# Decode tokens taken one block apart per stage, their attention on VectorE, a token-major mLSTM, and a weight stream of four split slots behind two raw ones

## The reference

```python
def hybrid_mixer(xn, conv_state, C0, n0, m0, w_in, b_in, conv_w, g_mh, w_out, chunk):
    proj = xn @ w_in + b_in
    gb, gc, hc, q, k, v, o, gates = jnp.split(proj, splits, axis=-1)
    y_conv, new_conv = short_conv(gc * hc, conv_state, conv_w)
    y_conv = gb * y_conv
    ...
    h, (C, n, m) = mlstm(qh, kh, vh, ig, lf, C0, n0, m0, chunk)
    h = h * lax.rsqrt(jnp.mean(h * h, axis=-1, keepdims=True) + EPS)
    y_ml = jax.nn.sigmoid(o) * (h * g_mh)
    out = jnp.concatenate([y_conv, y_ml], axis=-1) @ w_out
...
        hp = hp + mp
        hp = hp + cross_attn(rmsnorm(hp, g_cross[l]), pk, pv, w_xq[l], w_xo[l])
        hp = hp + swiglu(rmsnorm(hp, g_ffn[l]), w_gu[l], w_down[l])
```

## Time and profile before

| | |
|---|---|
| median of 3 runs | 3322.16 us (3309.95 to 3325.18) |
| the profiled execution | 3309.95 us |
| its span, first to last instruction | 3308.1 us |
| busy share: TensorE products, weight loads | 95%, 88% |
| VectorE, ScalarE, GpSimd | 51%, 39%, 45% |
| HBM traffic | 378.18 MB read, 13.30 MB written, 118 GB/s |

### The profile page before, as it was taken

The page is one execution under the profiler, slowest core; times in us unless marked ns, Lnnn a source line. Parts: engine busy times, 40 slices in busy tenths (PEclk is TensorE's granted clock), DMA queues, the critical chain, the costliest instruction groups (busy, mean ns, idle before and its releaser), DMA issues.

```text
span 3308.1 us, 42531 instructions
## 1 busy us (share of the span) xinstructions
PE 3148.3 (95%) x16970; PEld 2918.7 (88%) x16970; DVE 1671.9 (51%) x2695; ACT 1281.6 (39%) x2056; POOL 1489.7 (45%) x614
## 2 busy tenths in 40 slices
PE   8889999999899999889999998999999999999998
PEld 7888799988879999888799998888999888688886
DVE  6677532277754224677542267764224666542224
ACT  5444343344334334444343344344334444332222
POOL 1344355653434555434255553334655433244443
PEclk9999999999999999999999999999999999999999
DMA  5334233343423333334233343333333332122222
GB/s 211 108 123 142 90 122 126 128 137 120 136 97 118 124 130 124 129 129 142 79 126 127 128 143 120 117 122 117 126 128 124 131 121 90 52 94 97 96 102 89
DMA packets 132795, 394.24 MB, mean 119 GB/s; under 512 B 19812, under 2 KB 42340, under 8 KB 132472
## 3 DMA queue, kind: packets, MB, share of 16 engines
q1 hardware_dynamic: 99632, 350.87, 30.6%
q10 hardware_dynamic: 32968, 40.66, 3.9%
HBM read 378.18 MB, written 13.30 MB: 118 GB/s over the span
## 4 chain that ended last, share of the span: by engine, by line
PE 76%; DVE 14%; ACT 4%; issue 3%; DMA 2%; ACTq 1%; DVEq 0%; POOL 0%; SPq 0%
PE gb L312 67%; PE ta L473 2%; DMA o_sn<-work 1%; DVE r_res L1198 1%; DVE big L1091 1%; DVE big L1150 1%; DVE work L1114 1%; DVE work L1173 1%; PE tb L495 1%; PE td L495 1%; PE gm L505 1%; PE ta L521 1%; DVE x L1003 1%; ACT work L789 1%; DVE x L1189 1%
## 5 line engine op out<-in xcount | busy, mean ns | idle before, releaser
L294 POOL TENSOR_TENSOR w_lo<-w_raw,w_hi 128x1024 fp32r<-128x1024 f32 x610 | 1489.5, 2446 | 1791.8 <-ACT w_hi L604 1791.4
L312 PE MATMUL gb<-xn_hi,w_hi 128*128 128x386 f32 (+1 forms) x3280 | 1182.7, 361 | 15.5 <-DVE big L998 14.1
L312 PE MATMUL gb<-xn_hi,w_lo 128*128 128x386 f32 (+1 forms) x3280 | 1153.3, 352 | 0.0
L312 PE MATMUL gb<-xn_lo,w_hi 128*128 128x386 f32 (+1 forms) x3280 | 1152.8, 351 | 0.0
L604 ACT ACTIVATE w_hi<-w_raw 128x1024 fp32r<-128x1024 f32 x623 | 657.9, 1057 | 1223.3 <-PE gb L312 1171.5
L312 PEld LDWEIGHTS gb<-xn_hi,w_hi 128*128 128x128 f32 x3280 | 625.3, 191 | 51.2 <-issue 17.7
L312 PEld LDWEIGHTS gb<-xn_lo,w_hi 128*128 128x128 f32 x3280 | 625.4, 191 | 31.3 <-issue 2.2
L312 PEld LDWEIGHTS gb<-xn_hi,w_lo 128*128 128x128 f32 x3280 | 624.6, 190 | 26.2
L312 PE MATMUL gb<-act_hi,w_hi 128*128 128x386 f32 (+2 forms) x1648 | 575.8, 349 | 28.4 <-DMA mats<-mats_d 12.2
L312 PE MATMUL gb<-act_hi,w_lo 128*128 128x386 f32 (+2 forms) x1648 | 570.7, 346 | 0.0
L312 PE MATMUL gb<-act_lo,w_hi 128*128 128x386 f32 (+2 forms) x1648 | 570.7, 346 | 0.0
(11 more groups left out here) (199 smaller groups left out, 2476.3 us busy)
## 6 DMA issues: line engine op xcount, KB each, us to landing
w_raw<-w_st SPq DMA_DIRECT2D x610, 512.0 KB, 3.4
big<-kvc_d ACTq DMA_DIRECT2D x32, 512.0 KB, 4.5
big<-rows_d SPq DMA_DIRECT2D x16, 580.0 KB, 5.1
w_raw<-w_kv SPq DMA_DIRECT2D x16, 512.0 KB, 4.4
x<-x_blk SPq DMA_DIRECT2D x8, 772.0 KB, 6.9
y<-x ACTq DMA_DIRECT2D x16, 386.0 KB, 6.5
big<-x_blk ACTq DMA_DIRECT2D x24, 193.0 KB, 3.2
big<-rows_d SPq DMA_DIRECT2D x4, 768.0 KB, 5.2
```

Of the source, the lines that this page charges most:

```text
L294: pool.tensor_tensor(w_lo[:, g % NS, :], w_raw[:, g % NR, :], w_hi[:, g % NS, :].bitcast(F32), ALU.subtract).then_inc(w_lo_done, 1)
L312: mm = pe.matmul(gb[:, s, 0:wd], a[:, s, k * P:(k + 1) * P], r[:, k, 0:wd], start=(first and k == ks[0] and i == 0), stop=(last and k == k ...
```

## The change

- **Decode tokens.** All 8 go together, and one block later per stage: through the mixer's projections with block 1 (`DM`), its output and the queries with block 2 (`DO`), attention output and FFN with block 3 (`DX`). So each stage has one block of 392 columns, three of 384 and one of 512. Their mLSTM state update is done on VectorE and TensorE in block 1's FFN. Their attention is done on VectorE in block 2's FFN: 32 pieces (`dec_piece`), each a multiplication over 1,024 elements per partition and a sum, with the cache (1 MB for two pieces) and the broadcast query or probability rows loaded by SyncE between the weights.
- **Gates.** The two gate groups become one; a product with `pick` separates the forget gates. The four output-gate groups move ahead of the heads, with a sigmoid on ScalarE, so a block has 121 groups. The rows of the scans are turned into columns by `turn_rows`.
- **mLSTM token-major.** Numerator and normaliser come as 128 tokens by 129 columns: `n_part` has three products in place of five, the state is 129 columns wide with one update, the normaliser is one column per chunk, and `h_turn` transposes the result once per chunk, within the next head's q group.
- **Inputs scaled ahead.** `next_scale` multiplies the next block's input by the inverse norm in the third part of the FFN, so mixer groups need only a bias and ScalarE evacuates q, k, v, one convolution group and the gates (`take`).
- **Attention.** The steps of heads 2 and 3 move between the parts of the first three `O_XO` groups (`xo`); three output groups of the mixer are opened at once.
- **Slots.** `w_hi` and `w_lo` get 4 slots, `w_raw` 2, the product banks stay 3 (`NP`). The loads of the next block's input and the stores of `y` go from ScalarE's queue to SyncE's.

```diff
-BLK = [(3, 2), (3, 2), (3, 2), (3, 2), (4, 0)]
...
 NB = len(BLK)
+DM, DO, DX = 1, 2, 3
...
 O_GATE = 0
-O_HEAD = 2
-PER_HEAD = 7
+O_SIG = 1
+O_HEAD = O_SIG + HEADS
+PER_HEAD = 6
 O_OUT = O_HEAD + HEADS * PER_HEAD
...
-NS = 3
-NR = 3
+NS = 4
+NP = 3
+NR = 2
...
+G1, G2 = O_FF[1] - O_FF[0], O_FF[2] - O_FF[0]
+PIECE_AT = [2 * f + 1 for f in range(1, 8)] + [16 + m for m in range(8)] + [G1 + 1]
+PIECE_AT += [G1 + 11, G1 + 13] + [G1 + 14 + m for m in range(8)] + [G2 + 2 * f + 1 for f in range(6)]
...
+            def cache(i):
+                if i >= 2:
+                    sp.wait_ge(piece_done, 2 * (i - 2) + 2)
+                sp.dma_start(dcache[:, i % 2, :], kd_d[i] if i < NDEC else vd_d[i - NDEC]).then_inc(cache_loaded[i % 2], 16)
...
+            def piece_row(i):
+                if i >= 2:
+                    sp.wait_ge(piece_done, i - 1)
+                t, j = (i // 2) % NDEC, i % 2
+                if i < 2 * NDEC:
+                    src = qrow_d.rearrange("(k t) d -> t k d", t=NDEC)[t:t + 1, 4 * j:4 * j + 4, :].to_broadcast([P, 4, P])
+                    sp.dma_start(dbuf[:, j, :].rearrange("p (k d) -> p k d", k=4), src).then_inc(row_loaded[j], 16)
+                else:
+                    src = prow_d.rearrange("(t j) c -> t (j c)", t=NDEC)[t:t + 1, j * 512:(j + 1) * 512].to_broadcast([P, 512])
+                    sp.dma_start(dbuf[:, j, :], src).then_inc(row_loaded[j], 16)
...
+                if off == O_HEAD + 7 and b:
+                    store_y(b - 1)
...
+                    sp.wait_ge(y_lo, b * 8 + 8)
+                    for k in range(0, KT, 4):
+                        sp.dma_start(x_next[:, k:k + 4, 0:w],
+                                     x_blk[(b + 1) * KT + k:(b + 1) * KT + k + 4, :, 0:w].rearrange("k p c -> p k c")).then_inc(xnext_loaded, 16)
...
+                if b == DO:
+                    place = off - O_FF[0]
+                    if place == 0:
+                        sp.wait_ge(o_lo, b * 8 + 8)
+                        cache(0)
+                        cache(1)
+                    if place == 1:
+                        sp.wait_ge(qrow_stored, 16)
+                        piece_row(0)
+                        piece_row(1)
+                    for i in range(2, 4 * NDEC):
...
+                            if i >= 3:
+                                cache((i + 1) // 2)
+                    for i in range(2, 4 * NDEC):
+                        if place == max(PIECE_AT[i - 2] + 5, PROW_AT if i >= 2 * NDEC else 0):
+                            if i == 2 * NDEC:
+                                sp.wait_ge(prow_stored, 16)
+                            piece_row(i)
...
+                def pick_f():
+                    read_out(pe, gw(b, O_GATE))
+                    pe.matmul(td[:, 0:w_mix(b)], pick, gi[:, 0:w_mix(b)], start=True, stop=True).then_inc(f_picked, 1)
...
+                def turn_rows():
+                    pe.wait_ge(rows_exp, b + 1)
+                    for i, row in enumerate((a_row, row_g, row_e)):
+                        for c in range(CH):
+                            a = (i * CH + c) * HEADS
+                            mm = pe.matmul(tb[:, a:a + HEADS], row[:, c * P:(c + 1) * P], ident[:, 0:P:32], start=True, stop=True)
+                    mm.then_inc(col_t, 1)
...
+                def n_part(h, c):
...
+                    pe.matmul(bank[:, V1:2 * V1], w_sb[:, s, :], ktv[:, s, P:P + V1], start=True, stop=True)
+                    pe.matmul(bank[:, 2 * V1:3 * V1], ktv[:, s, 0:P], vs_sb[:, s, :], start=True, stop=True).then_inc(bu_done, 1)
+                    if c:
+                        pe.wait_ge(upd_done, j)
+                    elif b:
+                        pe.wait_ge(upd_done, ch0(b - 1, h + 1))
+                    old = state[:, h, :] if c == 0 else ws[:, c % 2, :]
+                    pe.matmul(bank[:, 0:V1], qf[:, c * P:(c + 1) * P], old, start=True, stop=True).then_inc(a_done, 1)
+                def h_turn(h):
...
+                    pe.wait_ge(hp_done, hd + 1)
+                    after(pe, yh_done, hd)
+                    for c in range(CH):
+                        mm = pe.transpose(gm[:, c * P:(c + 1) * P], hp[:, c, :], ident)
+                    mm.then_inc(ht_done, 1)
...
-                    def n_part(c):
...
-                        pe.matmul(tb[:, 0:P], ws[:, 0:P], qg[:, sl], start=True, stop=False)
-                        pe.matmul(tb[:, 0:P], ktv[:, s, P:2 * P], w_sb[:, s, :], start=False, stop=True)
-                        pe.matmul(tb[:, P:2 * P], ws[:, P:2 * P], qg[:, sl], start=True, stop=False)
-                        pe.matmul(tb[:, P:2 * P], ones, w_sb[:, s, :], start=False, stop=True)
-                        pe.matmul(tb[:, 2 * P:2 * P + V1], ktv[:, s, 0:P], vs_sb[:, s, :],
-                                  start=True, stop=True).then_inc(n_done, 1)
...
+                    q_hooks = {1: lambda: h_turn(h - 1)} if h else {6: turn_rows}
...
+                        c_hooks = {2: lambda: t_part(h, 0), 4: lambda: t_part(h, 1), 7: lambda: n_part(h, 0)}
+                        h_hooks = {1: lambda: t_part(h, 2), 3: lambda: n_part(h, 1), 7: lambda: n_part(h, 2)}
...
-                def dec_pv():
-                    pe.wait_ge(dpt_evac, b + 1)
-                    for half in range(2):
-                        for c in range(DEC * MT):
-                            i, mt = c // MT, c % MT
-                            mm = pe.matmul(ta[0:8, half, :], pz[:, mt, i, :], vc[:, c, half * 512:(half + 1) * 512],
-                                           start=(c == 0), stop=(c == DEC * MT - 1))
-                        mm.then_inc(dpv_done, 1)
...
+                def xo(i, h):
+                    gemm(gw(b, O_XO + i), W, act_hi, act_lo, (2 * h, 2 * h + 1), None if i else o_wait,
+                         first=h == 0, last=h == HEADS - 1)
+                xo(0, 0)
+                xo(1, 0)
+                ptrans(2)
+                xo(2, 0)
+                scores(3)
+                xo(0, 1)
+                xo(1, 1)
...
+                def take(g, dst, keep, **kw):
+                    act.wait_ge(group_done, g + 1)
+                    ps = gb[:, g % NP, :]
+                    func = kw.pop("func", ACT.Identity)
...
                 def q_high(m):
-                    read_out(gw(b, O_XQ + m))
+                    read_out(act, gw(b, O_XQ + m))
                     act.activation(act_hi[:, m, 0:TOK], q_att[:, (m // 2) % 2, m % 2, 0:TOK], ACT.Copy).then_inc(q_hi_done, 1)
...
+                    if m >= 2:
+                        w_high(gw(b, O_XQ + m))
...
+            def next_scale(b, e):
+                wd = w_mix(b)
+                v.wait_ge(r_done, r_mix_at(b))
+                v.scalar_tensor_tensor(out=x_next[:, e, 0:wd], in0=x_next[:, e, 0:wd], scalar=col(C_GMIX + e),
+                                       in1=r_mix[:, 0:wd], op0=ALU.mult, op1=ALU.mult).then_inc(mix_scaled, 1)
...
+                    def both(c):
+                        j = j0 + c
+                        bank = (tb, td)[j % 2]
+                        st(v.tensor_scalar(nd[:, c, :], bank[:, 0:V1], column(1, c, h), None, ALU.mult))
                         st.settle()
...
+                        v.tensor_tensor(nd[:, c, :], nd[:, c, :], bank[:, V1:2 * V1], ALU.add).then_inc(nd_done, 1)
...
+                def dec_piece(i):
...
+                    if i < 2 * NDEC:
+                        part = dcache[:, c % 2, :].rearrange("p (m d) -> p m d", m=MT)[:, :, j * 512:(j + 1) * 512]
+                        st(v.tensor_tensor(part, part, row.rearrange("p (o d) -> p o d", o=1).to_broadcast([P, MT, 512]), ALU.mult))
+                        st.settle()
+                        st(v.tensor_reduce(ds[:, :, t, 2 * j:2 * j + 2], part.rearrange("p m (h d) -> p m h d", h=2), AX.X, ALU.add))
+                        st.settle()
...
+                    v.sem_inc(piece_done, 1)
```

1573 lines of the change are left out of this document (830 added, 743 removed).

## The result

The changed kernel takes 3185.86 us (median of 4 runs, 3181.77 to 3188.35) where the kernel before takes 3319.03 (4 runs): a ratio of 0.960, with a 95% interval of 0.957 to 0.963. That is 4.0% faster. The forecast was 7.3% and 3080 us with a range of 3000 to 3175, so it went the right way, by a little over half of what was forecast, and ended 11 us above the range.

The account below looks back on a forecast made before the run. TensorE was taken to bound the kernel. From 3309.95 us, terms of -22.4, -28.6, -126, +1, -83, -10, +1, +24 and +12 summed to -232, giving 3078, rounded to 3080 us; range 3000 to 3175.

Parts of the forecast that it names:

- Widths: Products in all stages: 386 columns are paid like 392, so three blocks at 384 gain 3.3 ns a product, -28.6 us.
- Gates and heads: Mixer: one gate group less in each block, -22.4 us; heads -126 us over four blocks, +1 in block 4.
- `h_turn` wait: Heads: TensorE waits 1 us per head before the transposes of the result, 0 to 2 us in the profile.
- Attention: Queries and attention output: less time over the products, -83 us over four blocks (-115 to -47), -10 in block 4.
- So 30 against 50.8: Queries and attention output, per block: us over the products after against before, 19 of work plus 11 of waits.
- The softmax: Attention: 2.5 to 3.5 us from scores to transposes; six handovers with 0.5 to 3 us open, 11 us taken.
- Decode work: FFNs of blocks 1 and 2: TensorE's 8 us plus waits of 6 and 10 us, +24 (+8 to +85).
- Weight stream: SyncE's queue: weights still hidden with 1 us of margin; two or three delays a block, +12 us (0 to +60).
- the rival of late weights: Weight loads: rows and caches between weights wait for VectorE, +30 to +120 with the stores, 3110 to 3200 us; chance 0.17.
- Start: Kernel's start: third weight waits for a raw slot, scaling ahead saves about 4 us; +1 us (0 to +12).

Follow-up runs that it names:

- runs 1 and 9: Changed kernel with the squares' additions three tiles later, 3127.99 us; changed kernel with the mixer's output opening two groups, not three, 3167.76 us.
- run 2: Changed kernel with the softmax's negation and scaling moved from VectorE to ScalarE: 3149.60 us.
- run 7: Changed kernel with the loads of the decode work later on SyncE's queue, all work done: 3150.56 us.
- Runs 3 and 4: Changed kernel without the decode attention pieces in block 2's FFN, 3153.49 us; then also without their cache and row loads, 3143.03 us.
- run 6: Changed kernel with ScalarE copying the memory's values ahead of the last three high parts at the start: 3184.67 us.
- run 8: Changed kernel with squares' additions late, softmax steps on ScalarE, start reordered, decode loads later, and maxima of heads 1 and 2 ahead of the query tile: 3043.60 us.

## Why the prediction was wrong

- **Widths: right.** Products of 384 columns cost 173.4 ns (137.84 us for 795 on the chain) and of 392 177.3 (108.53 for 612), against the 173.3 and 176.7 taken. The straight line that the Trainium skill gives for a lone product ("TensorE: Matmul & The Clock Gate", Back-to-back issue gap) would have made this term 0. The rows of either trace are 11 to 13 ns above it, and 386 costs what 392 does.

```profile
490.08 137.84 PE gb L449 x795
...
2172.81 108.53 PE gb L449 x612
```

- **Gates and heads: right, and 37 us too small.** With the gates and the mixer's output 194 us went, of which 156 were forecast. In block 1 the four output-gate groups and the heads take some 141 us, inside the 139 to 145 that the prediction names. No `h_turn` wait is in the list, so the 4 us per block for it was too much, and the window shows 1.4 us without TensorE at work in 120.41. The mixer's output, for which nothing but the widths was forecast, went from 197.5 to 184.4 us over the blocks; block 4 gave most of the rest.
- **Attention: the step that failed first.** "So 30 against 50.8", 19 of work and 11 of waits, measured 43 to 47. Two of its prices failed. The passes for the values were put at 0.173 us, the price of a product in fp32r. Full float32 passes of 384 columns start 0.32 us apart at full granted clock, so 32 of them take 10.3 per block for 5.5; they did so in the kernel before too, in the row at 317.50 below. And three groups opened together were costed at nothing: the residual rows behind them, priced in the earlier trace rows at 1,792 ns for the squares alone, had no slack to give (runs 1 and 9). That cost waits of 3.4 to 3.7 us and half clock at the openings of four blocks, half of them in the FFN. In block 1, 14.7 us over the forecast, the passes are 4.8 of it, the queries' opening 6.5, the clock after head 2's wait some 3, and two small waits (L1312, L1363) 1.8; the rest took some 1.5 us less than estimated. A head's passes for the values before, then with the change:

```profile
317.50 1.45 PE L495 MATMUL tb<-work,mem_v 128*128 128x384 f32 x4
```

```profile
1521.48 1.45 PE L617 MATMUL td<-big,mem_v 128*128 128x384 f32 x4
1522.77 1.45 PE L617 MATMUL tb<-big,mem_v 128*128 128x384 f32 x4
1523.77 0.63 PE L449 MATMUL gb<-act_hi,w_hi 128*128 128x384 f32 x1
```

- **The softmax: right in sum, by luck.** The waits before the transposes come to 11.1 us in block 1, and 11 were taken for all waits. But the chain put at 2.5 to 3.5 us takes 5.0 to 8.7 in the blocks of 384, and TensorE waits at four handovers, not six. GpSimd's subtraction, moved off the query's subtraction (L1363 now 703 ns on average, near the 0.6 us forecast), met VectorE's next small steps in place of it, and head 2's maxima stood behind a query tile. So the 36 us of run 2, but for their part in the clock, lie within what the forecast had allowed for waits, and are not what it missed.
- **Decode work: mechanism right, size off.** Forecast +24; measured 77 us over the products in the FFNs of blocks 1 and 2 beyond the 2.4 of before, of which 14 are openings that block 0's FFN has too: 63. A piece lasts 2.75 us (1.53 and 1.22), at the low end of the 2.6 to 5 estimated; what was missed is that the loads' places make SyncE wait (run 7), and that VectorE's other steps there fall more often on GpSimd's subtractions: the hidden tile's product takes 1,841 ns there, and 833 in block 1's FFN. Runs 3 and 4 split the 39 us that block 2's FFN lost without them (316.9 to 277.6) into about 25 for the pieces and 15 for the loads.
- **Weight stream: right where it was looked for, wrong where it was not.** FFNs without decode work show no wait for `w_lo`, so the +12 was not needed there; the rival of late weights held at the decode loads alone, and reached ScalarE's residual rows and hidden tiles through its order. In block 2's FFN a weight lands in 4.1 us at the median, under the 4.4 that the prediction had named for that rival, but in up to 9.6. It is a part of the miss, not the whole: the order of the loads gave 35 us, that of the residual rows 58.
- **Start: +13 for +1.** ScalarE's copies of the values stand behind high parts that wait for the scaling; run 6 took back 2.6 us of it in the trace. The rest was not followed.

With the edits of run 8 the kernel takes 3043.6 us, 36 under the 3080 forecast, and queries with attention output (494.7 us over the blocks) and FFN (1531.0) lie within 10 us of their forecast sums. The passes cost what they did, and some of the decode work's price stays; what makes up for it is that the waits before the transposes fall to 2.9 us in a block, where 11 were forecast.

## What to carry to other kernels

When groups are opened together to hide one wait, look at what consumes them: three that end at once put the consumer two groups behind, and an engine whose tile takes 98% of a group's time does not catch up within eight of them. Put what TensorE needs (the split row) ahead of what is only summed, and each load on a queue where its wait is already over when the queue, not the consumer, gets there. Moving a step away from a collision with a neighbour engine moves the collision: follow the neighbour's 2.4 us to the instruction that it meets next, and take from that engine what stands on the chain. Price an instruction by its own rows, not by those of a neighbour of the same shape: the float32 passes cost nearly twice an fp32r product.

## What the hardware showed that was not expected

The stall beside GpSimd hits the smallest instruction as hard as the largest: a 128x2 multiplication on VectorE went from at most 169 ns to as much as 2,207, while the reductions and reciprocals next to it stayed at 0.69 and 0.16 us. The Trainium skill ("SBUF — State Buffer", Who interferes with whom) says that an operation of one input and a scalar can use the port pair that VectorE shares with GpSimd, and is blocked for GpSimd's whole instruction where that holds the pair first, while a reduction is not. The rows agree: the 2.37 us scaling at 286.55 began behind the subtraction at 286.41. And a single wait of 3.7 us on a busy TensorE was followed by 6 us at a granted clock of 0.50, so that the wait counted nearly twice.
